# Filling TensorE's waits between the out-projection and the experts with identity products

## The reference

```
hn = rms_norm(x, g1);  proj = hn @ w_in
att = sliding-window attention with sinks (8 heads, 2 kv heads)
h_m = mLSTM, 4 heads, chunkwise, with conv, gates and norm
x = x + concat(att, h_m) @ w_out
t = rms_norm(x, g2)
grp = argmax(t @ w_rg + b_rg)            # 4 groups
top-2 of softmax over the group's 4 experts (t @ w_re + b_re)
x = x + sum over the 2 chosen experts of weight * (silu(t @ w_gate) * (t @ w_up)) @ w_down
```

## Time and profile before

| | |
|---|---|
| median of 3 runs | 1065.3 us (1063.83 to 1066.48) |
| profiled execution | 1064.2 us |
| its span, first to last instruction | 1062.4 us |
| mean granted TensorE clock | 0.947 |
| TensorE matmuls | busy 948.8 us (89%), 5026 records |
| TensorE weight loads | 792.8 us (75%), 5027 |
| VectorE | 618.2 us (58%) |
| ScalarE | 527.4 us (50%) |
| GpSimd | 246.2 us (23%) |

### The profile page before, as it was taken

One profiled execution on the slowest core, in us unless ns is written; L12 is line 12 of the kernel. 1 busy time (PEld: TensorE's weight loads), 2 busy tenths in 40 slices (PEclk: granted clock), 3 DMA queues, 4 the chain that ended last, 5 costly groups with the idle time before them and its releaser, 6 DMA issues. The chain is left out here.

```text
span 1062.4 us, 16918 instructions
## 1 busy us (share of the span) xinstructions
PE 948.8 (89%) x5026; PEld 792.8 (75%) x5027; DVE 618.2 (58%) x1245; ACT 527.4 (50%) x945; POOL 246.2 (23%) x362
## 2 busy tenths in 40 slices
PE   4789999999999969699971799999999999999993
PEld 3678889898888857588861577877877777787772
DVE  3646555656665565343367466447639489754891
ACT  3364644627455373122114356545638488664871
POOL 3101001010110100000017133243234345513452
PEclk9999999999999986899985799999999999999998
DMA  8620010101000050533463788678669799966963
GB/s 259 216 54 20 22 40 0 39 0 39 20 20 20 2 190 9 172 126 134 142 220 102 288 285 255 166 231 289 177 202 339 220 319 395 374 174 202 321 245 60
DMA packets 58122, 169.68 MB, mean 160 GB/s; under 512 B 12744, under 2 KB 15088, under 8 KB 58096
## 3 DMA queue, kind: packets, MB, share of 16 engines
q1 hardware_dynamic: 50384, 143.13, 37.5%
q0 software_dynamic: 7712, 26.24, 10.5%
HBM read 142.96 MB, written 26.38 MB: 159 GB/s over the span
## 5 line engine op out<-in xcount | busy, mean ns | idle before, releaser
L886 PE MATMUL bank_j<-w_high,rows_high 128*128 128x512 f32 x640 | 256.6, 401 | 11.7 <-DVE w_low L1327 9.4
L888 PE MATMUL bank_j<-w_high,rows_low 128*128 128x512 f32 x640 | 251.4, 393 | 0.0
L887 PE MATMUL bank_j<-w_low,rows_high 128*128 128x512 f32 x640 | 251.3, 393 | 0.0
L886 PEld LDWEIGHTS bank_j<-w_high,rows_high 128*128 128x128 f32 x640 | 121.2, 189 | 40.9 <-issue 12.3
L525 POOL TENSOR_TENSOR tick<-mhalf 1x1 f32<-1x1 f32 x146 | 83.9, 577 | 279.1 <-ACT lg L823 136.8
L888 PEld LDWEIGHTS bank_j<-w_high,rows_low 128*128 128x128 f32 x640 | 121.2, 189 | 26.1
L887 PEld LDWEIGHTS bank_j<-w_low,rows_high 128*128 128x128 f32 x640 | 121.6, 190 | 23.7
L1632 DVE TENSOR_TENSOR w_low<-w_res,w_high 128x1024 fp32r<-128x1024 f32 x96 | 112.8, 1219 | 13.8 <-ACT w_high L633 13.8
L633 ACT ACTIVATE w_high<-w_res 128x1024 fp32r<-128x1024 f32 x96 | 96.2, 1059 | 8.4 <-PE bank_j L888 8.0
L880 PE MATMUL bank_t<-ident,hn 128*128 128x128 f32 x328 | 45.1, 283 | 33.8 <-DMA hn<-ffn_in,row_g 22.2
L880 PEld LDWEIGHTS bank_t<-ident,hn 128*128 128x128 f32 x328 | 40.0, 146 | 39.0 <-issue 34.8
(11 more groups left out here) (301 smaller groups left out, 1823.0 us busy)
## 6 DMA issues: line engine op xcount, KB each, us to landing
w_res<-in_w_gate_dram SPq DMA_DIRECT2D x48, 512.0 KB, 4.9
w_res<-in_w_up_dram SPq DMA_DIRECT2D x48, 512.0 KB, 5.4
bias<-in_w_down_dram SPq DMA_DIRECT2D x32, 512.0 KB, 5.6
slot_b<-in_w_gate_dram SPq DMA_DIRECT2D x16, 512.0 KB, 5.7
PT<-in_w_up_dram SPq DMA_DIRECT2D x16, 512.0 KB, 5.9
gmix<-in_w_down_dram SPq DMA_DIRECT2D x16, 512.0 KB, 5.5
h<-in_w_down_dram SPq DMA_DIRECT2D x16, 512.0 KB, 7.2
hn<-in_x_dram SPq DMA_DIRECT2D x8, 512.0 KB, 3.5
```

The lines of the kernel that those rows point to most:

```text
L886: pe.matmul(out_, ah, bh, start=start, stop=False)
L887: pe.matmul(out_, ah, bl, start=False, stop=False)
L888: return pe.matmul(out_, al, bh, start=False, stop=stop)
```

## The change

TensorE's stream gets a helper, `keep_clock(n)`, which issues n products of the 128x128 float32 identity with itself into the first 128 columns of the bank T0, each with start and stop, without a wait and without a semaphore. It is called three times: 30 products behind the loop of stage two (after `router(6)`, ahead of `h2_T(7)`), 12 behind `router(7)` (ahead of `positions(2, 2)`), and 80 behind `positions(2, 2)` (ahead of the wait for `dve_tab` and of `rows_T(0)`). No other engine's code is changed.

```diff
@@ -1106,6 +1106,11 @@
                     ins = pe.matmul(X0[:, 0:NG + NE], h2T[:, k, :], wr[:, k, :], start=(k == 0), stop=(k == KC - 1))
                 ins.then_inc(pe_r, 1)
 
+            def keep_clock(n):
+
+                for _ in range(n):
+                    pe.matmul(T0[:, 0:P], ident[:, :], ident[:, :], start=True, stop=True)
+
             def body2(t, u, first, last):
                 if not first:
                     project_out(t, u, 0)
@@ -1124,10 +1129,12 @@
             pe.wait_ge(dve_C, TILES)
             pe.wait_ge(ld_wr, 32)
             tiles2(pe, body2)
+            keep_clock(30)
             h2_T(TILES - 1)
             router(TILES - 1)
+            keep_clock(12)
             positions(2, 2)
-
+            keep_clock(80)
 
 
             pe.wait_ge(dve_tab, 1)
```

## The result

| | before | after |
|---|---|---|
| median | 1065.89 us (4 runs, 1063.83 to 1067.88) | 1076.55 us (4 runs, 1076.02 to 1077.78) |
| profiled execution | 1064.2 us | 1076.02 us |
| its span | 1062.4 us | 1074.2 us |
| mean granted TensorE clock | 0.947 | 0.952 |

The ratio is 1.0102, interval 1.0080 to 1.0124. The change costs 10.7 us. The forecast was 4.4 us slower, 1069.7 us, with a range up to 1073.8: the sign is right and the size is not.

The account below looks back on a forecast made before the run. It took the chain through `desti` and GpSimd's routing to the experts, at the low clock, as the bound. Later `desti` 5.4, other fills 0, minus 0.5 and 0.5 gave +4.4 us: 1069.7 us, range 1066.4 to 1073.8.

Parts of the forecast that it names:

- What comes back at once: Behind the first fill, transposes and `router(7)` at the high clock return 2.66 us, making `desti` 5.4 us later (4.4 to 7.6).
- The sum: Total over the whole kernel: 5.4 + 0 + 0 - 0.5 - 0.5 = +4.4 us, from +1.3 to +8.3.
- First fill: 30 products between `router(6)` and `h2_T(7)`: 9.1 us long, `h2_T(7)` 8.0 us late.
- The cheap fill: Rival: reloading the same weight makes fill records 0.058 us each; +1.0 us in all, 1066.3; chance 0.06.
- Second fill: 12 products before `positions(2, 2)`, in a 4.87 us idle stretch: cost 0, bound 0.7 us.
- Third fill: 80 products behind `positions`: 19.8 us, hidden behind GpSimd's chain with 2.4 us left before the gathered rows.
- What the warm clock gives: Before and at the experts: clock low again at their start; 0.5 us back in transposes, 0.5 us at the experts.
- The rival in which it is held: Clock stays high from the third fill to the experts, which start at 2.4 GHz: +2.3 us, 1067.6; chance 0.20.
- The path: From `desti` through GpSimd's scatters and gather to the experts: ends last by 0.36 us, passing any `desti` delay on in full.
- the rival that made it faster: At GpSimd's copy of `row_g`: the shifted table load meets a VectorE pause, 5.6 us back; -1.2 us; chance 0.05.
- the clock that never rises: Identity products in the fills never raise the clock; third fill sticks out: +28.5 us, 1093.8; chance 0.05.
- what I wrote that the profile would show: Signs: `h2_T(7)` near 563, clock rise 556.5 to 558.8, thirteenth scatter near 576 released by `desti`, expert matmuls 0.43 us apart.

Follow-up runs that it names:

- g1_signals_all: The changed kernel with every fifth product of all three fills raising a semaphore nobody waits for: 1067.89 us, ratio 1.0040 to the kernel before.
- g4_third_only: The changed kernel without the first two fills, 86 products behind `positions`, nine behind the gather's transposes, every fifth signalling: 1060.61 us, ratio 0.9977 to before.
- i1: The kernel of g4_third_only (86 products behind `positions`, nine behind the gather's transposes) with no signal in the fills: 1060.74 us, ratio 0.9971 to before.
- h3: The changed kernel with its first fill replaced by 60 unsignalled float32r products of 128x256, one record each, without the identity: 1080.58 us (1 run).
- h4: The changed kernel with a single signal, at the 15th of the first fill's 30 products, answered by nobody: 1074.07 us (1 run).
- g2_every_15: The changed kernel with signals at the 15th and 30th product of the first fill, each answered by ScalarE: 1068.40 us (1 run).
- e1: The changed kernel with the first fill left out, second and third kept without signals: 1068.99 us, ratio 1.0025 to before.
- e4: The changed kernel with 15 products in the first fill instead of 30: 1068.61 us (1 run).
- h2: The changed kernel with a first fill of 25 products signalling every fifth, then 30 without signals: 1078.85 us (1 run).

## Why the prediction was wrong, point by point

**The step that failed** is "What comes back at once". It let the transposes and `router(7)` follow the fill at the high clock, with 2.66 us back, and `desti` 5.4 us later. It took for granted that the signal behind the transposes is on time, as in every row of before. The sum has no term for it. In its place the runs showed a signal 4.67 us late, the clock fallen in that wait, and no 1.72 us back in the router; only the transposes' 0.93 came. Its upper bound, 7.6 us, had the router slow again but not the wait that makes it slow, so the range ended 2.8 us short of the median.

**The rest of the step is right once the signal is on time.** In g1_signals_all `desti` is 4.25 us later, forecast 5.4 with a lower bound of 4.4, so the fill's price was set too high, by some 1.1 us; and the time is 4.5 us longer (2.6 to 6.0 by the interval), forecast 4.4. That the two agree so closely is luck: the trace has only 2.8 us of it from `router(6)` on. But the forecast was the price of the mechanism that it described, and not that of the kernel.

**First fill.** 9.1 us forecast, 8.21 measured (lower bound 8.2): the clock rose after 2.7 us and not 3.5, and a record took 0.112 us at the high level and 0.213 at the low one, and not 0.124 and 0.232. `h2_T(7)` was 6.83 us late instead of 8.0. Of the two prices in the earlier trace rows the lower one, 0.116 from the accumulating stream, was the nearer. The Trainium skill's 81 ns (TensorE: Matmul & The Clock Gate, section "Back-to-back issue gap") is not what these float32 records take. (The prediction puts its effect at 2.5 us, which is a fill at the high clock throughout; for the forecast's own 45 fast records it is 45 x 0.043, an estimated 1.9 us by that page's figure.) The cheap fill, at 0.058 us a record, fell too.

**Second fill.** 5.39 us in a gap of 4.87, at the low clock, within its bound of 0.7. Since `positions` was shorter, nothing of it is left at `desti`.

**Third fill.** Hidden, as forecast, and shorter: 18.11 us instead of 19.8. Both are at the high clock throughout, since it had risen at 579.6, just before the fill; the difference is the record's price, 0.112 us and not 0.124. 4.53 us were left before the gather, where 2.4 were forecast.

**What the warm clock gives.** The clock was low at the experts, as forecast; 0.5 us came back there and none in the transposes. The rival in which it is held fell. g4_third_only shows what that needed: 1.5 us of gap instead of 4.5, and products in the wait for `rows_low`. There the Trainium skill's advice to keep gaps between bursts short (TensorE: Matmul & The Clock Gate, section "Why this matters for your kernels") is borne out; I had argued from a gap of 2.4 us, and by the trace it was twice that.

**The path.** That `desti` ends last and hands its delay on in full is right: 10.42 us at `desti`, 10.45 at the first expert matmul. The copy of `row_g` stayed at 5.77 us, so the rival that made it faster fell, and so did the clock that never rises. Of what I wrote that the profile would show, `h2_T(7)`'s 1.03 us, the rise, the releaser of the thirteenth scatter and the 0.43 us matmuls are there. The thirteenth scatter "near 576" stands at 583.55: 2.5 us of that lie ahead of `router(6)`, and 5.0 are the missed term.

**What stays open.** Shown is that the lateness behind the first fill comes with the row of 60 small records and goes when every fifth product signals, with the same products in the same order. Not shown is what holds TensorE up. It is not the clock's change inside the row alone (i1), not float32 or the identity (h3), not missing signals alone (i1, and the convolution's row before), not the burst of loads alone (g1, and the same row), and a single signal in the middle is not enough (h4). How many signals are needed, whether the answers of ScalarE helped in g2_every_15, whether the burst of loads or GpSimd's scatters beside the fill matter, and whether the profiler's recording, which loses events in just these executions, has a part in it or causes it, was not tried.

## What to carry to other kernels

In this kernel keep-warm products belong only where they end before the next real work can start: behind `positions` they returned 0.2 to 0.3% in g4 and i1, ahead of `h2_T(7)` they cost their own length less what the clock returns, even with every signal on time. They pay when they reach to within some 1.5 us of that work and bridge the waits behind it too; a fill that ended 4.5 us too early returned 0.5 us. And check in the trace that the first signal behind a long row of small products arrives when its record ends: compare the waiting copy's start with that end, and look for "remote" as the releaser.

## What the runs showed of the hardware

- A completion signal of TensorE can arrive several microseconds after the end of its record, in recorded executions: 4.67 (twice), 4.73, 4.63, 7.38 and 7.11 us behind 60 records, and 5.06 us behind `positions` in e1. In e1, e4 and h2 TensorE's timeline also has holes of 0.3 to 1.8 us at "issue". The seven kernels with a signal on every fifth product of the first fill or of all their fills never showed it; in h2, where 30 products without signals follow 25 with them, the fifth signal was 0.84 us late.
- It goes with lost events: the nine traces that show it lack 11 to 41 events of semaphores, the other eleven none or one. Which of the two brings the other is not known.
- Products of the identity raise the clock from 1.2 to 2.4 GHz: it rose 2.7 us after the first fill began, which followed `router(6)` at once, and in g4 3.2 us after a fill that followed 4.87 us of idle time and the four records of `positions`.
- A float32 product of 128x128 takes 0.223 us at 2.4 GHz in a row of its like (1.115 us for five), two records each; at 1.2 GHz a record took 0.213 us.
